# Expert biases loaded early, the last output tile in column halves, three low parts on VectorE, and a shorter way to the first expert

## The chip, the cores and the metric

The kernel runs on one core of a Trainium2 chip. The core has five engines with queues of their own: TensorE (PE), VectorE (DVE), ScalarE (ACT), GpSimd (POOL) and SyncE (SP, which here only issues transfers), and 16 DMA engines that serve all queues. The metric is the device time of one execution in microseconds (us). Of this kernel, runs agree within some 0.5%: three runs before the change took 1217.61, 1223.28 and 1223.31 us.

## The reference

One decoder layer on 256 tokens of width 1024, in float32:

```python
h = rms_norm(x, g_attn);  proj = h @ w_in
# proj -> native sparse attention (8 heads) and forgetting attention (8 heads)
y = merge[:, :, 0] * (o_nsa @ w_up_nsa) + merge[:, :, 1] * (o_fox @ w_up_fox)
x = x + y @ w_out
x = x + moe_ffn(rms_norm(x, g_mlp), ...)

def moe_ffn(...):                       # 32 experts, top 4 per token
    logits = xt @ w_router + b_router
    top_val, top_idx = top_k(logits, 4);  top_w = softmax(top_val)
    for each expert:                    # w_g, w_u, w_d are 1024 x 1024 each
        g = minimum(xt @ wg + bg, 7.0);  u = clip(xt @ wu + bu, -7.0, 7.0)
        y = ((u + 1.0) * g * sigmoid(1.702 * g)) @ wd + bd
        acc += combine[expert] * y
```

The expert weights are 32 x 3 matrices of 4 MB, 403 MB in all. Everything else that is read is some 35 MB.

## The kernel before, in words

The work is one long program for each engine, in an order written by hand; semaphores tie the engines together.

**Attention part (to about 250 us).** Every weight block is split into a high part (float32r, made by ACT, `keep_high`) and a low part (the rest, `keep_low`, line 357). A product is three TensorE passes: high by high, low by high, high by low. The low parts of the six projection blocks are made by POOL and DVE in turns. From the merge gates on, pieces are numbered (`MERGE`, `UP`, `OUT`), and their low parts are all made by POOL in the order of the numbers. `low_done(j)` is the semaphore value that says that the pieces below `j` have their low parts.

**Output product.** `y @ w_out` has eight pieces of the inner dimension (`OUT+0` to `OUT+7`), each for two tiles of 128 tokens (t = 0, 1) and two column halves (h = 0, 1); a piece of one tile is six matmuls with 512 columns (`out_piece`). Pieces 0 to 3 are done for both tiles; then pieces 4 to 7 for tile 0, then for tile 1. `w_hi` and `w_lo` hold four pieces, so ACT makes the high part of piece 4 only when TensorE has used piece 0 (`out_used`), and so on. Before `OUT+3` ACT issues eight transfers that bring the gate and up biases of the 32 experts (64 KB each) into `heads`, which is in use until then. After `OUT+7` ACT waits for them and makes `bias_hi`; DVE makes `bias_parts` from it and goes on to `x` only after that.

**From the output to the first expert.** DVE adds the output to `x` (line 1027), TensorE transposes the sums (`turn_rows`), DVE copies the transposes times a gain into `hT` (line 784), TensorE makes the router's logits (line 1457), ACT and POOL make the norm's factors and ACT scales `xn`. DVE then picks the top four (lines 1038 to 1062), TensorE counts with triangular matrices how many earlier tokens chose each expert (lines 1472 to 1476), DVE makes `route` and the one-hot matrices `hot`, and TensorE gathers the rows of the first two experts (`gather`, line 1486). Three calls of `keep_warm` put dummy matmuls (14, 10 and 4) ahead of steps that wait. Then DVE makes the number of rounds (`total_i`, `route_made`), reads it into a register (line 1179), and copies the gathered rows (`keep_x`, line 1159), on which the first expert's first product waits (`ex_made`).

**Experts.** For each expert TensorE does gate, up and down products, each in two halves of the inner dimension (`product`, line 1502), and scatters the rows back. Expert `it` begins with gate half 0; the down product of expert `it - 1` comes between the gate halves.

**Expert weights.** A half matrix is 2 MB. The 192 halves go through a ring of eight slots, issued by SP (line 408) in a fixed order. The first eight have no earlier expert to wait for, but the attention part uses the same slots, so `ex_freed` gives for each of these places what must be over: place 0 the turned outputs, place 1 `low_done(OUT)`, place 2 the merged `y`, place 3 `low_done(OUT + 4)`, place 4 `low_done(OUT + 8)`, places 5 to 7 the whole output product (`out_done` 2). Place 8 and all later ones wait until TensorE has used the slot: place 8 for half 0 of the first gate product.

Of the kernel before, what the change touches and what calls it, by code (L numbers as in the profile page):

```python
# [31 lines left out]
P = 128  # L32
# [11 lines left out]
E = 32  # L44
# [26 lines left out]
def build(nc, a, out):  # L71
    with ExitStack() as ctx:
# [3 lines left out]
        def sem(name):  # L76
            return ctx.enter_context(nc.semaphore(name))
# [50 lines left out]
        e_sel = sb("e_sel", [P, 2, 2 * C], F32R)  # L128
        sel_cols = sb("sel_cols", [P, 2, E])
# [40 lines left out]
        e_bias = heads[:, 1024:2048].rearrange("p (m n) -> p m n", m=2)  # L170
        bias_hi = oT_hi[:, 0:2].rearrange("p a b t -> p (a b t)").rearrange("p (m n) -> p m n", m=2)
        bias_parts = oT_lo[:, 0:2].rearrange("p a b t -> p (a b t)").rearrange("p (m n) -> p m n", m=2)
# [48 lines left out]
        rv0 = route[:, 0:8]  # L221
# [36 lines left out]
        bias_hi_made, bias_made, sel_ready, gain_in = map(sem, ("bias_hi_made", "bias_made", "sel_ready", "gain_in"))  # L258
        hotw_made, hotw_turned, hotT_made = sem("hotw_made"), sem("hotw_turned"), sem("hotT_made")
# [59 lines left out]

        def low_done(j):  # L320

            return (lo_made, j - N_SPLIT // 2)
# [6 lines left out]
        ex_freed = [(o_turned, 4), low_done(OUT), (y_made, KD), low_done(OUT + 4), low_done(OUT + KD)] + [(out_done, 2)] * 3  # L329
# [52 lines left out]
        def _(sp):  # L382
# [27 lines left out]
            def expert_head(first, end):  # L410

                for m, h in HEAD[first:end]:
                    sp.wait_ge(vrow_set, 1)
                    sp.wait_ge(*ex_freed[ex_place(m, h, 0, True)])
                    load_half(m, h, 0, ex_place(m, h, 0, True))

            def expert_body(base, u):

                it = base + u
                if isinstance(it, int):  # L420
                    e, e_before, now, prev = it, it - 1, it, it - 1
                else:
                    e = sp.snap(sp.to_reg(it & (E - 1)), min_val=0, max_val=E - 1)
                    e_before = sp.snap(sp.to_reg((it - 1) & (E - 1)), min_val=0, max_val=E - 1)
                    now, prev = sp.to_reg(it), sp.to_reg(it - 1)
                freed_by = [(half_done["up"], prev), (mat_done["up"], prev), (half_done["gate"], now),
                            (half_done["down"], prev), (mat_done["down"], prev), (mat_done["gate"], now)]
                for i, (m, h, back) in enumerate(BODY):
                    place = ex_place(m, h, u - back)
                    first = isinstance(it, int) and it == 1  # L430
                    if first and place < EX_SLOTS:
                        sp.wait_ge(*ex_freed[place])
                    elif first and (m, h) == ("up", 0):
                        sp.wait_ge(half_done["gate"], 1)
                    else:
                        sp.wait_ge(*freed_by[i])
                    load_half(m, h, e_before if back else e, place)
            for i, (name, pieces, k, n) in enumerate(BLOCKS):
                if name == "out1":
                    expert_head(0, 1)  # L440
                if name == "cv1":
                    sp.wait_ge(squared, NT)
                elif in_ring.index(name) >= len(RING):
                    for user in freed[in_ring[in_ring.index(name) - len(RING)]]:
                        sp.wait_ge(*user)
                if i:
                    load(name, pieces)

# [28 lines left out]
        def _(pool):  # L477
# [84 lines left out]
            for j in range(N_SPLIT, N_PIECES):  # L562
                keep_low(pool, nc.gpsimd, j, lo_made)
# [5 lines left out]
        def _(act):  # L569
# [189 lines left out]
        def _(dve):  # L759
# [250 lines left out]
            keep_low_y(KD - 1)  # L1010

# [9 lines left out]
            nc.vector.scalar_tensor_tensor(out=bias_parts, in0=bias_hi, scalar=less_hi[:, 0:1], in1=e_bias,  # L1021
                                           op0=ALU.mult, op1=ALU.add).then_inc(bias_made, 1)

            for t in range(NT):
                dve.wait_ge(out_done, 1 + t)
                for h in range(2):
                    last = nc.vector.scalar_tensor_tensor(out=x[:, t, 512 * h:512 * h + 512], in0=(S, TB)[t][h][:, :], scalar=0.5,
                                                          in1=x[:, t, 512 * h:512 * h + 512], op0=ALU.mult, op1=ALU.add)
                last.then_inc(summed, 1)
                keep_hT_tile(R_GM, [PJ[0], PJ[1], OB[0], OB[1]], 4, t)  # L1030
            for t in range(NT):
                dve.wait_ge(squared, NT + t + 1)
                inv_rms(rr[:, t:t + 1], ss[:, t:t + 1], D)


# [29 lines left out]
            dve.wait_ge(pos_done, 1)  # L1065
            for t in range(NT):
                last = nc.vector.scalar_tensor_tensor(out=above[:, t, :], in0=TB[1][:, E * t:E * t + E], scalar=1.0,
                                                      in1=chosen[:, t, :], op0=ALU.add, op1=ALU.mult)
            step(last)
# [5 lines left out]
            step(last)  # L1075
            for t in range(NT):
                for i in range(2):
                    last = nc.vector.tensor_scalar(hot[:, t, i, :], slot_no[:, :], rv0[:, 4 * i + t:4 * i + t + 1], None, ALU.is_equal)
                last.then_inc(hot_made, 1)
# [4 lines left out]
            step(nc.vector.tensor_reduce(tot[:, 0:1], TB[1][:, 2 * E:3 * E], AX.X, ALU.max))  # L1084
# [93 lines left out]
            dve.wait_ge(route_made, 1)  # L1178
            total = dve.value_load(total_i[0:1, 0:1], min_val=E, max_val=ROUNDS * E)
# [4 lines left out]
            expert(0, 0, True)  # L1184
            for u in range(1, STEPS):
                expert(u, u, False)
# [8 lines left out]
        def _(pe):  # L1195
# [233 lines left out]
            def out_piece(kk, t):  # L1429
                q, w = slice(P * t, P * t + P), quarter(OUT + kk)  # L1430
                for h in range(2):
# [12 lines left out]
            for t in range(NT):  # L1444
                for kk in range(4, KD):
                    if t == 0:
                        pe.wait_ge(*low_done(OUT + kk + 1))
                    elif kk == KD - 1:
                        pe.wait_ge(summed, 1)
                        turn_rows(x, 0, turned_banks)  # L1450
                    last = out_piece(kk, t)
                last.then_inc(out_done, 1)

            def router(t):

                for k in range(KD):
                    last = mm(PJ[0][:, E * t:E * t + E], hT[:, k, P * t:P * t + P], w_r[:, k, :], start=(k == 0), stop=(k == KD - 1))
                last.then_inc(lg_done, 1)
            pe.wait_ge(hT_made, 6)
            router(0)  # L1460
# [8 lines left out]
            keep_warm(14)  # L1469
# [4 lines left out]
            mm(TB[1][:, E:2 * E], before[:, :], chosen[:, 1, :], start=False, stop=True)  # L1474
            mm(TB[1][:, 2 * E:3 * E], ones[:, :], chosen[:, 0, :], start=True, stop=False)
            mm(TB[1][:, 2 * E:3 * E], ones[:, :], chosen[:, 1, :], start=False, stop=True).then_inc(pos_done, 1)
# [155 lines left out]
```

## Time and profile before

| | |
|---|---|
| runs before | 1217.61, 1223.28, 1223.31 us; median 1223.28 |
| profiled execution | 1221.0 us, span 1219.3 us |
| TensorE | busy 1123.5 us (92%), granted clock 0.986 of full |
| DVE, ACT, POOL | busy 430.5 (35%), 175.6 (14%), 133.0 us (11%) |
| DMA, slices 10 to 39 of 40 (305 to 1189 us) | 407 to 430 GB/s |
| DMA, slices 3 to 8 (91 to 244 us) | 69 to 162 GB/s |
| DMA, slices 9 and 10 (244 to 305 us) | 355 and 285 GB/s |
| chain that ended last | PE 48%, DMA 42%, DVE 7% |

The page cuts the span into 40 slices of 30.5 us. "Busy" of TensorE is pipelined and says little of its limit; the DMA rate by slice and the chain of waits say more. The profiled execution took 1.7 us more than its span.

### The profile page before, as it was taken

What the parts mean: (1) busy time and instruction counts of PE and PEld (TensorE: products, weight loads), DVE (VectorE), ACT (ScalarE), POOL (GpSimd) and SP (SyncE); (2) the same over time, 40 slices, a digit from 0 to 9 for tenths busy, and PEclk for the clock granted to TensorE, in tenths of its full rate; (3) what the DMA queues carried; (4) which work ended last, traced back from release to release, by engine and by line L of the source; (5) the groups of instructions that cost most, each with busy time, mean ns of one, the idle gap of its engine ahead of it and who ended that gap; (6) DMA issues with size and microseconds to landing.
All of it is one profiled execution on the core that took longest, in us unless ns stands there. A gap on an engine that the chain in (4) does not pass through costs nothing.

```text
span 1219.3 us, 14702 instructions
## 1 busy us (share of the span) xinstructions
PE 1123.5 (92%) x5812; PEld 543.6 (45%) x5812; DVE 430.5 (35%) x891; ACT 175.6 (14%) x363; POOL 133.0 (11%) x123
## 2 busy tenths in 40 slices
PE   4998999989999999999999999999999999999997
PEld 3776899866333343333333333333333333333332
DVE  4674575634232323223222322222322222222222
ACT  3452444422000000000000000000000000000000
POOL 4562344650000000000000000000000000000000
PEclk9997999999999999999999999999999999999999
DMA  8842232297999999999999999999999999999995
GB/s 268 274 162 69 70 120 89 81 355 285 415 407 428 428 428 427 428 428 428 427 429 430 427 428 427 429 430 429 426 427 429 429 430 428 427 428 429 429 430 233
DMA packets 49423, 438.81 MB, mean 360 GB/s; under 512 B 6538, under 2 KB 13774, under 8 KB 24814
## 3 DMA queue, kind: packets, MB, share of 16 engines
q1 hardware_dynamic: 47364, 437.44, 86.3%
q10 hardware_dynamic: 2026, 0.92, 0.3%
q8 instruction: 22, 0.36, 0.1%
q14 instruction: 11, 0.09, 0.0%
HBM read 437.30 MB, written 1.05 MB: 360 GB/s over the span
## 4 chain that ended last, share of the span: by engine, by line
PE 48%; DMA 42%; DVE 7%; issue 1%; ACT 1%; POOL 1%; SPq 1%; ACTq 0%; DVEq 0%
PE bank L1502 28%; DMA ring<-in_w_e_up_dram 20%; DMA ring<-in_w_e_gate_dram 20%; PE bank L1486 3%; PE bank L1516 2%; DVE w_lo L357 2%; DMA heads<-in_b_e_up_dram 1%; PE bank L1498 1%; PE bank L1372 1%; PE bank L1373 1%; PE bank L1371 1%; PE bank L1536 1%; PE bank L1340 1%; POOL small L549 1%; PE bank L1226 1%
## 5 line engine op out<-in xcount | busy, mean ns | idle before, releaser
L1502 PE MATMUL bank<-ring,hT 128*64 128x512 f32 x2048 | 466.9, 598 | 20.3 <-DMA ring<-in_w_e_gate_dram 19.5
L1502 PEld LDWEIGHTS bank<-ring,hT 128*64 128x64 f32 x2048 | 137.6, 136 | 302.2 <-issue 256.9
L1502 PE MATMUL bank<-ring,heads 128*64 128x512 f32 x1024 | 229.6, 601 | 0.6 <-DVE heads L1142 0.6
L1175 DVE TENSOR_TENSOR x<-x,bank 128x512 f32<-128x512 f32 x128 | 82.3, 684 | 143.9 <-PE bank L1516 143.9
L1502 PEld LDWEIGHTS bank<-ring,heads 128*64 128x64 f32 x1024 | 71.3, 138 | 136.9 <-issue 129.3
L1124 DVE TENSOR_SCALAR heads<-bank 128x512 f32<-128x512 f32 x32 | 22.1, 692 | 308.3 <-PE bank L1502 308.3
L357 POOL TENSOR_TENSOR w_lo<-ring,w_hi 128x512 fp32r<-128x512 f32 (+2 forms) x64 | 111.4, 1763 | 99.0 <-ACT w_hi L600 98.9
L733 ACT ACTIVATE work<-bank 128x256 f32<-128x256 f32 x32 | 12.3, 385 | 501.0 <-PE bank L1529 501.0
L1516 PE MATMUL bank<-heads,work 64*128 64x512 f32 x256 | 72.8, 641 | 1.5 <-ACT heads L738 0.8
L600 ACT ACTIVATE w_hi<-ring 128x512 fp32r<-128x512 f32 (+2 forms) x88 | 61.3, 723 | 29.6 <-PE bank L1235 16.1
L1486 PE MATMUL bank<-work,xn 128*128 128x128 f32 x528 | 64.5, 275 | 0.0
L1486 PEld LDWEIGHTS bank<-work,xn 128*128 128x128 f32 x528 | 61.6, 192 | 0.8 <-issue 0.8
L1498 PE MATMUL bank<-oT_lo,e_sel 128*128 128x512 f32 x64 | 31.6, 494 | 25.4 <-DMA ring<-in_w_e_gate_dram 22.1
L1142 DVE COPY heads<-bank 128x512 f32<-128x512 f32 x32 | 22.1, 692 | 90.1 <-PE bank L1536 90.1
L738 ACT ACTIVATE heads<-bank 128x512 f32<-128x512 f32 x32 | 19.1, 597 | 221.4 <-PE bank L1502 221.4
L1130 DVE TENSOR_SCALAR heads<-bank 128x512 f32<-128x512 f32 x32 | 22.1, 692 | 78.5 <-PE bank L1502 78.5
L1498 PEld LDWEIGHTS bank<-oT_lo,e_sel 128*128 128x128 f32 x64 | 11.9, 186 | 77.7 <-DMA ring<-in_w_e_gate_dram 29.0
L1516 PEld LDWEIGHTS bank<-heads,work 64*128 64x128 f32 x256 | 19.6, 184 | 53.9 <-issue 52.0
L745 ACT ACTIVATE heads<-heads 128x512 f32<-128x512 f32 x32 | 20.2, 630 | 152.8 <-DVE heads L1124 152.8
L1371 PE MATMUL bank<-hT_hi,w_hi 128*128 128x256 f32 x128 | 39.9, 311 | 0.0
L1372 PE MATMUL bank<-hT_lo,w_hi 128*128 128x256 f32 x128 | 36.9, 289 | 0.0
L1373 PE MATMUL bank<-hT_hi,w_lo 128*128 128x256 f32 x128 | 36.9, 288 | 0.0
(275 smaller groups left out, 1063.5 us busy)
## 6 DMA issues: line engine op xcount, KB each, us to landing
ring<-in_w_e_gate_dram SPq DMA_DIRECT2D x64, 2048.0 KB, 33.6
ring<-in_w_e_up_dram SPq DMA_DIRECT2D x64, 2048.0 KB, 35.2
ring<-in_w_e_down_dram SPq DMA_DIRECT2D x64, 2048.0 KB, 34.8
ring<-in_w_in_dram SPq DMA_DIRECT2D x8, 2048.0 KB, 7.9
ring<-in_w_out_dram SPq DMA_DIRECT2D x2, 2048.0 KB, 8.3
ring<-in_w_in_dram SPq DMA_DIRECT2D x2, 1024.0 KB, 9.0
ring<-in_w_ck_dram SPq DMA_DIRECT2D x1, 2048.0 KB, 8.5
heads<-in_w_cv_dram SPq DMA_DIRECT2D x1, 2048.0 KB, 14.1
```

The costliest lines, as they stand in the source:

```text
L357: last = vec.tensor_tensor(w_lo[:, k, n], w, w_hi[:, k, n], ALU.subtract)
L600: last = nc.scalar.activation(w_hi[:, k, n], w, ACT.Copy)
L1124: nc.vector.tensor_scalar(e_g, banks[1][:, :], LIMIT, None, ALU.min).then_inc(g_made, 1)
L1130: nc.vector.tensor_scalar(e_u, banks[2][:, :], LIMIT, -LIMIT, ALU.min, ALU.max).then_inc(up_read, 1)
L1175: ins = nc.vector.tensor_tensor(x[:, t, 512 * h:512 * h + 512], x[:, t, 512 * h:512 * h + 512], bank67[:, j % 2, :], ALU.add)
L1371: mm(PJ[c % 2][:, 0:T], w_hi[:, k, w], hT_hi[:, k, :], start=(k == 0), stop=False)
L1372: mm(PJ[c % 2][:, 0:T], w_hi[:, k, w], hT_lo[:, k, :], start=False, stop=False)
L1373: last = mm(PJ[c % 2][:, 0:T], w_lo[:, k, w], hT_hi[:, k, :], start=False, stop=(k == KD - 1))
L1486: last = mm(banks[0][:, P * k:P * k + P], xn[:, t, c:c + P], hot[:, t, :, :].rearrange("p u s -> p (u s)"), start=(t == 0), stop=(t == NT ...
L1498: mm(bank[:, :], e_sel[:, u % 2, :], bias_parts[:, (m == "up") * 1, :], start=True, stop=False)
L1502: last = mm(bank[C * half:C * half + C, :], lhs(kk), w[:, k, 512 * half:512 * half + 512], start=(kk == 0 and m == "down"), stop=(kk == KD ...
L1516: mm(bank67[:, h, :], hotT[C * h:C * h + C, t, :], e_y[C * h:C * h + C, :], start=True, stop=True).then_inc(spread_done, 1)
```

## The change

- The expert biases get a place of their own, `e_bias`, which shares its memory with `bias_parts`. SP issues their eight transfers behind the block `fk`, at some 35 us. ACT makes `bias_hi` after the high part of `OUT+5`, not after `OUT+7`.
- The low parts of `OUT+3`, `OUT+5` and `OUT+7` are made by DVE (between its other steps there), the rest by POOL. `low_done` and `ex_freed` name the right semaphores: place 3 now waits for POOL's and DVE's parts, and so does place 4.
- Tile 1 of the output is done in column halves: pieces 4 to 7 of half 0 (`last_half`), then the transposes of tile 0, then pieces 4 to 7 of half 1. DVE adds half 0 while TensorE works on half 1. The transposes and router products of tile 1 go by halves as well.
- `keep_warm` is called with 8, 3 and 2 dummy matmuls in place of 14, 10 and 4.
- `above` is made in one instruction, and `hot` from it in two, ahead of `route`. The count that only the number of rounds needs goes to another bank with a semaphore of its own (`load_counted`).
- TensorE no longer waits for `route_made` before the transposes of `comb`, and TensorE and DVE read the number of rounds after the first expert.

```diff
+        with ExitStack() as parts:
+            bias_parts = parts.enter_context(nc.sbuf_tensor("bias_parts", [P, 2, 512], F32R))
+        e_bias = sb("e_bias", [P, 2, 512])
...
+        LOW_BY_VECTOR = [OUT + 3, OUT + 5, OUT + 7]
+
         def low_done(j):
 
-            return (lo_made, j - N_SPLIT // 2)
+            piece, by_vector = j - 1, sum(v < j for v in LOW_BY_VECTOR)
+            if piece in LOW_BY_VECTOR:
+                return (lo_made_v, N_SPLIT // 2 + by_vector)
+            return (lo_made, j - N_SPLIT // 2 - by_vector)
...
-        ex_freed = [(o_turned, 4), low_done(OUT), (y_made, KD), low_done(OUT + 4), low_done(OUT + KD)] + [(out_done, 2)] * 3
+        ex_freed = [[(o_turned, 4)], [low_done(OUT)], [(y_made, KD)], [low_done(OUT + 3), low_done(OUT + 4)],
+                    [low_done(OUT + 7), low_done(OUT + 8)]] + [[(out_done, 2)]] * 3
...
+                if name == "fk":
+                    for q in range(4):
+                        for m, bias in enumerate(("b_e_gate", "b_e_up")):
+                            sp.dma_start(e_bias[E * q:E * q + E, m, :],
+                                         a[bias][0][:, 512 * (q // 2):512 * (q // 2) + 512]).then_inc(ebias_in, 16)
...
             for j in range(N_SPLIT, N_PIECES):
-                keep_low(pool, nc.gpsimd, j, lo_made)
+                if j not in LOW_BY_VECTOR:
+                    keep_low(pool, nc.gpsimd, j, lo_made)
...
             for kk in range(3, KD):
                 if kk == 3:
                     act.wait_ge(up_done, KD)
-
-                    for q in range(4):
-                        for m, name in enumerate(("b_e_gate", "b_e_up")):
-                            act.dma_start(e_bias[E * q:E * q + E, m, :],
-                                          a[name][0][:, 512 * (q // 2):512 * (q // 2) + 512]).then_inc(ebias_in, 16)
                 else:
                     act.wait_ge(out_used, kk - 3)
                 keep_high(OUT + kk)
-
-            act.wait_ge(ebias_in, 16 * 8)
-            nc.scalar.activation(bias_hi, e_bias, ACT.Copy).then_inc(bias_hi_made, 1)
-
-            for t in range(NT):
-                act.wait_ge(summed, t + 1)
+                if kk == 5:
+                    act.wait_ge(ebias_in, 16 * 8)
+                    nc.scalar.activation(bias_hi, e_bias[:, :, :], ACT.Copy).then_inc(bias_hi_made, 1)
+
+            for t in range(NT):
+                act.wait_ge(summed, (1, 3)[t])
                 square_rows(t)
...
+            keep_low(dve, nc.vector, OUT + 5, lo_made_v)
             dve.wait_ge(bias_hi_made, 1)
...
+            keep_low(dve, nc.vector, OUT + 7, lo_made_v)
...
+            dve.wait_ge(out_done, 1)
+            add_out(0, 0)
+            add_out(0, 1).then_inc(summed, 1)
+            dve.wait_ge(last_half, 1)
+            add_out(1, 0).then_inc(summed, 1)
+            out_banks = [PJ[0], PJ[1], OB[0], OB[1]]
+            keep_hT_tile(R_GM, out_banks, 4, 0)
+            dve.wait_ge(squared, NT + 1)
+            mean_of(0)
+            dve.wait_ge(out_done, 2)
+            add_out(1, 1).then_inc(summed, 1)
+            keep_hT_tile(R_GM, out_banks, 4, 1)
+            dve.wait_ge(squared, NT + 2)
+            mean_of(1)
+            dve.wait_ge(inv_made, n_inv[0])
...
+            for t in range(NT):
+                nc.vector.scalar_tensor_tensor(out=hot[:, t, :, :], in0=slot_no[:, :].unsqueeze(1).to_broadcast([P, 2, C]), scalar=1.0,
+                                               in1=above[:, t, 0:2].unsqueeze(2).to_broadcast([P, 2, C]),
+                                               op0=ALU.add, op1=ALU.is_equal).then_inc(hot_made, 1)
...
-            dve.wait_ge(route_made, 1)
-            total = dve.value_load(total_i[0:1, 0:1], min_val=E, max_val=ROUNDS * E)
             dve.wait_ge(gain_in, 16)
             keep_x(-1, -1)
             dve.wait_ge(comb_turned, 1)
             nc.vector.tensor_copy(combT, bank45[0:E, 1, T:2 * T].rearrange("p (t q) -> p t q", t=NT)).then_inc(combT_made, 1)
             expert(0, 0, True)
+            dve.wait_ge(route_made, 1)
+            total = dve.value_load(total_i[0:1, 0:1], min_val=E, max_val=ROUNDS * E)
...
+            for kk in range(4, KD):
+                pe.wait_ge(*low_done(OUT + kk + 1))
+                last = out_piece(kk, 0)
+            last.then_inc(out_done, 1)
+            for kk in range(4, KD):
+                last = out_piece(kk, 1, (0,))
+            last.then_inc(last_half, 1)
...
+            pe.wait_ge(summed, 1)
+            turn_sums(0, 0)
+            turn_sums(0, 1)
+            for kk in range(4, KD):
+                last = out_piece(kk, 1, (1,))
+            last.then_inc(out_done, 1)
...
             pe.wait_ge(summed, 2)
-            turn_rows(x, 1, turned_banks)
-            pe.wait_ge(hT_made, 8)
-            router(1)
+            turn_sums(1, 0)
+            router(0, 0)
+            pe.wait_ge(summed, 3)
+            turn_sums(1, 1)
+            router(0, 1).then_inc(lg_done, 1)
+            router(1, 0)
+            router(1, 1).then_inc(lg_done, 1)
...
-            keep_warm(14)
+            keep_warm(8)
...
-            keep_warm(10)
+            keep_warm(3)
             gather(2, 0, True)
             pe.wait_ge(comb_made, 1)
-            pe.wait_ge(route_made, 1)
...
-            keep_warm(4)
+            keep_warm(2)
             expert(0, 0, True)
+            pe.wait_ge(route_made, 1)
```

## Rows read from the trace of the kernel before

**Rows 1.** Windows: us, busy by engine, TensorE clock, DMA share, GB/s; steady stage.

```profile
356.00:576.00 220.00, 220.00 (x1053) 81.22 (x1049) 65.28 (x129) 13.75 (x26) 0.00 (x0) 1.00 1.00 427
```

**Rows 2.** The same view around the output product and the first expert.

```profile
252.00:268.00 16.00, 12.73 (x53) 9.26 (x52) 0.60 (x4) 4.96 (x5) 11.76 (x5) 1.00 1.01 356
...
294.00:296.00 2.00, 2.00 (x12) 0.43 (x7) 0.00 (x0) 0.00 (x0) 0.00 (x0) 1.00 0.00 0
```

**Rows 3.** Timeline of SP's queue: start us, us, line, transfer, count.

```profile
265.44 0.33 SPq L408 DMA_DIRECT2D ring<-in_w_e_gate_dram  x1
275.40 0.80 SPq L408 DMA_DIRECT2D ring<-in_w_e_down_dram  x2
...
296.21 6.82 SPq L408 DMA_DIRECT2D ring<-in_w_e_up_dram  x2
```

**Rows 4.** Timeline of ACT, output stage.

```profile
252.52 3.90 ACT L600 ACTIVATE w_hi<-ring 128x1024 fp32r<-128x1024 f32 x4 [3.30 <-issue]
...
269.25 1.06 ACT L714 ACTIVATE oT_hi<-heads 128x1024 fp32r<-128x1024 f32 x1 [8.97 <-DMA heads<-in_b_e_up_dram]
```

**Rows 5.** Timeline of POOL, output stage.

```profile
253.66 11.76 POOL L357 TENSOR_TENSOR w_lo<-ring,w_hi 128x1024 fp32r<-128x1024 f32 x5 [2.64 <-ACT w_hi L600]
```

**Rows 6.** Timeline of DVE, output stage.

```profile
242.00 2.52 DVE L996 TENSOR_TENSOR hT_lo<-heads,hT_hi 128x256 fp32r<-128x256 f32 x1
...
270.35 1.28 DVE L1021 SCALAR_TENSOR_TENSOR oT_lo<-oT_hi,less_hi,heads 128x1024 fp32r<-128x1024 f32 x1 [17.68 <-ACT oT_hi L714]
```

**Rows 7.** Timeline of TensorE, output stage.

```profile
246.17 0.40 PE L1434 MATMUL bank<-w_hi,hT_hi 128*128 128x512 f32 x1
...
254.13 0.39 PE L1436 MATMUL bank<-w_lo,hT_hi 128*128 128x512 f32 x1
256.18 0.47 PE L1434 MATMUL bank<-w_hi,hT_hi 128*128 128x512 f32 x1 [1.66 <-POOL w_lo L357]
...
272.89 1.09 PE L1203 MATMUL bank<-ident,x 128*128 128x128 f32 x8 [1.68 <-DVE x L1027]
```

**Rows 8.** Chain that ended last, router and dummy matmuls: start us, us, what.

```profile
275.37 1.71 PE bank L1457 x16
...
278.93 2.40 PE bank L1457 x16
281.33 4.40 PE bank L1468 x28
```

**Rows 9.** Timeline of DVE, expert choice.

```profile
281.45 0.41 DVE L1038 SCALAR_TENSOR_TENSOR work<-bank,small 128x32 f32<-128x32 f32 x2 [1.69 <-PE bank L1457]
...
283.92 0.23 DVE L1055 TENSOR_TENSOR work<-small,work 128x64 f32<-128x64 f32 x1
...
286.89 0.29 DVE L1067 SCALAR_TENSOR_TENSOR small<-bank,work 128x32 f32<-128x32 f32 x2 [1.77 <-PE bank L1476]
...
288.98 0.19 DVE L1084 TENSOR_REDUCE small<-bank 128x1 f32<-128x32 f32 x1
```

**Rows 10.** Timeline of TensorE, gather of the first two experts.

```profile
288.92 1.95 PE L1486 MATMUL bank<-work,xn 128*128 128x128 f32 x16
```

**Rows 11.** Chain that ended last, DVE ahead of the first expert, and the first products.

```profile
290.35 0.55 DVEq L1179
...
291.34 0.70 DVE hT L1159
...
292.08 0.50 PE bank L1498
```

**Rows 12.** Windows (columns of Rows 1) in which TensorE's clock was low.

```profile
110.00:112.00 2.00, 2.00 (x11) 2.00 (x11) 0.39 (x2) 0.00 (x0) 0.00 (x0) 0.50 0.00 0
...
280.00:282.00 2.00, 2.00 (x13) 2.00 (x13) 0.51 (x3) 2.00 (x2) 0.40 (x1) 0.57 1.00 426
```

**Rows 13.** Timelines of SP and ACT, projection stage.

```profile
35.00 11.98 SPq L388 DMA_DIRECT2D ring<-in_w_in_dram  x2
...
56.79 5.42 ACT L600 ACTIVATE w_hi<-ring 128x512 fp32r<-128x512 f32 x8 [8.53 <-PE bank L1235]
```

More of the change, by code:

```diff
@@ L431, in expert_body @@
                     if first and place < EX_SLOTS:
-                        sp.wait_ge(*ex_freed[place])
+                        for user in ex_freed[place]:
+                            sp.wait_ge(*user)
                     elif first and (m, h) == ("up", 0):
@@ L1010, in _ @@
             keep_low_y(KD - 1)
+            keep_low(dve, nc.vector, OUT + 3, lo_made_v)
             step(nc.vector.tensor_reduce(sel_cols[:, :, :], ident[:, :].rearrange("p (h q e) -> p h e q", h=2, q=2), AX.X, ALU.add))
@@ L1065, in _ @@
             dve.wait_ge(pos_done, 1)
+            step(nc.vector.scalar_tensor_tensor(out=above[:, :, :], in0=TB[1][:, 0:NT * E].rearrange("p (t e) -> p t e", t=NT),
+                                                scalar=1.0, in1=chosen, op0=ALU.add, op1=ALU.mult))
             for t in range(NT):
-                last = nc.vector.scalar_tensor_tensor(out=above[:, t, :], in0=TB[1][:, E * t:E * t + E], scalar=1.0,
-                                                      in1=chosen[:, t, :], op0=ALU.add, op1=ALU.mult)
-            step(last)
+                nc.vector.scalar_tensor_tensor(out=hot[:, t, :, :], in0=slot_no[:, :].unsqueeze(1).to_broadcast([P, 2, C]), scalar=1.0,
+                                               in1=above[:, t, 0:2].unsqueeze(2).to_broadcast([P, 2, C]),
+                                               op0=ALU.add, op1=ALU.is_equal).then_inc(hot_made, 1)
             steps = ROUNDS * E
@@ L1074, in _ @@
                                                col(round_off[:, :], E), ALU.add)
[L1075 to L1079, printed above, removed]
             for t in range(NT):
@@ L1427, in _, with out_piece @@
             turned_banks = [PJ[0], PJ[1], OB[0], OB[1]]
-            def out_piece(kk, t):
+            def out_piece(kk, t, halves=(0, 1)):
                 q, w = slice(P * t, P * t + P), quarter(OUT + kk)
-                for h in range(2):
+                for h in halves:
                     ps = (S, TB)[t][h][:, :].rearrange("p (a b) -> p a b", b=P)
@@ L1443, in _, with turn_sums, router @@
             pe.wait_ge(yT_lo_made, KD)
[L1444 to L1456, printed above, removed]
+            for kk in range(4, KD):
[5 more added lines that the diff above has]
+            last.then_inc(last_half, 1)
+            def turn_sums(t, j):
+                for k in range(4):
+                    c = P * (4 * j + k)
+                    last = nc.tensor.transpose(turned_banks[2 * t + j][:, P * k:P * k + P], x[:, t, c:c + P], ident[:, :])
+                last.then_inc(xn_turned, 1)
+            pe.wait_ge(summed, 1)
[4 more added lines that the diff above has]
+            last.then_inc(out_done, 1)
+            def router(t, j):
+                pe.wait_ge(hT_made, 4 + 2 * t + j + 1 if t else 6)
+                for k in range(4 * j, 4 * j + 4):
                     last = mm(PJ[0][:, E * t:E * t + E], hT[:, k, P * t:P * t + P], w_r[:, k, :], start=(k == 0), stop=(k == KD - 1))
-                last.then_inc(lg_done, 1)
-            pe.wait_ge(hT_made, 6)
-            router(0)
+                return last
             pe.wait_ge(summed, 2)
-            turn_rows(x, 1, turned_banks)
-            pe.wait_ge(hT_made, 8)
-            router(1)
+            turn_sums(1, 0)
[5 more added lines that the diff above has]
+            router(1, 1).then_inc(lg_done, 1)
             def keep_warm(n):
@@ L1473, in _ @@
             mm(TB[1][:, E:2 * E], ones[:, :], chosen[:, 0, :], start=True, stop=False)
-            mm(TB[1][:, E:2 * E], before[:, :], chosen[:, 1, :], start=False, stop=True)
-            mm(TB[1][:, 2 * E:3 * E], ones[:, :], chosen[:, 0, :], start=True, stop=False)
-            mm(TB[1][:, 2 * E:3 * E], ones[:, :], chosen[:, 1, :], start=False, stop=True).then_inc(pos_done, 1)
+            mm(TB[1][:, E:2 * E], before[:, :], chosen[:, 1, :], start=False, stop=True).then_inc(pos_done, 1)
+            mm(S[1][:, 0:E], ones[:, :], chosen[:, 0, :], start=True, stop=False)
+            mm(S[1][:, 0:E], ones[:, :], chosen[:, 1, :], start=False, stop=True).then_inc(load_counted, 1)
             def gather(n, half, newest):
```

27 lines of the change are left out of this document (12 added, 15 removed).

## The prediction, made before the change was run

> **What bounds the kernel now.** I read the DMA rates by slice first. From 305 us to the end the rate stands at 407 to 430 GB/s, while TensorE, at 92% busy, says little. The stage view of 356 to 576 us has both: TensorE without a gap and the DMA engines at a share of 1.00 and 427 GB/s [rows 1]. So a 2 MB half matrix takes 2.097 MB / 427 GB/s = 4.9 us, an expert of six halves 29.5 us, and 184 halves from place 8 on take some 904 us. The end hangs on when that stream starts and how long it then stands still; TensorE only follows it. This makes every microsecond by which the stream restarts earlier a microsecond of the result, and no work after the restart changes.
>
> Next, the view of SP's queue shows where the stream stands still. SP issues place 4 at 265.44, places 5 to 7 at 275.40 and the two behind, and place 8 at 296.21 [rows 3]. Three halves need 3 x 4.9 = 14.7 us, so the queue is empty again at some 292; in 294 to 296 us the share is 0.00 [rows 2]. What SP waits for at place 8 is the first half of expert 0's gate product. Thus the path that sets the end runs, before 296, over the engines: from the output product to that gate half.
>
> The chain of waits and the engines' timelines give that path. ACT begins the high part of `OUT+3` at 252.52, after 3.30 us of issuing [rows 4]; POOL makes the five last low parts in 11.76 us, 2.35 each [rows 5]; TensorE waits for them at 256.18 for 1.66 us and less later [rows 7]. ACT waits 8.97 us for the bias transfers, until 269.25, and DVE, behind it, 17.68 us until 270.35 [rows 4, 6]. TensorE waits for DVE's sum 1.68 us until 272.89 [rows 7]. Then follow router, choice, counts, gather, and DVE's copy at 291.34, on which the first product at 292.08 waits [rows 8 to 11].
>
> **The change, part by part.** I follow one path, output product to gate half 0, and give each step's new time. TensorE's start at 246.17 rests on steps that stay.
>
> *High parts.* ACT's transfers, 3.30 us of issuing, go; the high part of `OUT+3` starts at about 249.2 in place of 252.52. Each takes 3.90 / 4 = 1.0 us. The others wait for `out_used`: TensorE's 36 matmuls from 246.17 to 254.4 are 0.228 us each, so a piece of both tiles (12 matmuls) is 2.73 us, and pieces 0 to 3 end at 248.9, 251.6, 254.4 and 257.1 when nothing waits [rows 7]. The high parts of `OUT+4` to `OUT+7` are there at some 251.5, 252.8, 255.5 and 258.2, the bias's high part at 253.9.
>
> *Low parts.* DVE's price for one is not in this trace. The nearest row is its 1024-column instruction with two inputs in SBUF, 1.28 us [rows 6]; POOL's 2.35 is the other end. But DVE also stands: at 242.00 an instruction of 256 columns took 2.52 us while POOL worked on a low part of 1024 columns [rows 6]. I take 1.28 and let each wait for the other's whole instruction. DVE does `OUT+3` at 251.6 to 252.8 (behind its last `yT` low part); POOL `OUT+4` to 255.3; DVE `OUT+5` to 256.5; POOL `OUT+6` to 258.9; DVE the bias parts to 260.1 and `OUT+7` to 261.3. The page "SBUF — State Buffer" of the Trainium skill, section "Who interferes with whom", says that a VectorE instruction with two SBUF inputs and a GpSimd one that reads SBUF shut each other out for whole instructions. Row and rule agree on DVE's side; the rule speaks against this part of the change: without it `OUT+7` would be there at 259.5, with it at 261.3.
>
> *Output product.* TensorE needs `OUT+4` at 257.1, `OUT+5` at 258.5, `OUT+6` at 259.8 and `OUT+7` at 261.2. Only the last is late, by 0.2. Tile 0 ends at 262.8. Half 0 of tile 1 (12 matmuls, 2.73), eight transposes (1.09) and half 1 (2.73) follow without a wait, since DVE's two additions are over at 264.2: the whole product ends at 269.35. Before, it ended with SP's issue at 275.40 [rows 3]. This is 6.0 earlier. Of DVE's price the bounds are: 0.7 less cost gives 0.2, 2.35 with the lock 1 to 3 us later.
>
> *Router.* Eight transposes 1.09 and 32 passes at 1.71 for 16 make 4.5, so the logits can be read at 273.95. DVE's additions and copies of tile 1 end at 272.2 and hide behind the router; the factor of tile 1 is there at 272.9. Before, the second router block took 2.40 rather than 1.71, and it waited for `hT` [rows 8]; DVE read at 281.45 [rows 9]. 7.5 earlier.
>
> *Choice and counts.* From 281.45 to the end of line 1055 are 2.7 us, so `chosen` is there at 276.7. The 28 passes of dummies, 4.40 us from 281.33, kept TensorE until 285.7, 1.5 beyond that point [rows 8, 9]. Eight calls are 16 passes of 0.11 to 0.16, over at 275.7 to 276.4: the wait for them goes. Six passes of counts take 0.75, and DVE begins `above` at 277.65, behind `comb`; before 286.89. 9.2 earlier. `hot` now stands ahead of `route` (0.6 us saved) and takes two instructions for four: done at 278.7. `xn` is done at 275.4 and hides. TensorE's three dummies end at 278.7 as well. The gather of 1.95 runs 278.7 to 280.7; before it began at 288.92 [rows 10]. 10.2 earlier.
>
> *To the first product.* DVE still has `route` and the chain of small instructions to do, 1.05 and the 1.37 between 288.98 and 290.35, which ends at 281.1; the register read of 0.9 us between 290.35 and 291.34 goes from here [rows 9, 11] and lies in DVE's free time behind expert 0. The copy takes 0.70, so the first product starts at 281.9 in place of 292.08: 10.2 earlier. What is late next is DVE's chain, by 0.3 over the gather.
>
> *The transfers.* Gate half 0 ends at 286.0, and place 8 is issued there and not at 296.21. Places 5 to 7, issued at 269.4, are served until 286.0, by the 16.6 us from issue to the empty queue of before. So the stream has caught up just when place 8 comes: the DMA engines bound the gain at about 11. The early issue of biases costs SP the 3.3 us of issuing that ACT spent [rows 4], behind `fk`, at 35.0, and SP has nothing to issue until 46.6; the high part of `fk` starts at 56.79 [rows 13]. Even 4 us later `fk` would be there. Cost nothing; without that cover, up to 4. Their leaving the output stage gives more: 252 to 268 us ran at 356 and not 427 GB/s [rows 2], (1 - 356/427) x 16 = 2.7 us of transfer time, which is what lets places 5 to 7 find a free queue.
>
> *Sum.* 1221.0 us of the profiled execution (span 1219.3 and 1.7 around it) less 10.2 is 1210.8; I say 1211. The median of the runs is 2.3 above that execution and the fastest 3.4 below, and I keep this spread in the range.
>
> **The rivals.**
>
> *The clock falls in the first expert.* At 280 to 282 us the granted clock was 0.57 [rows 12], after gaps of TensorE at 272 and 278 (the router waits in rows 7 and 8): 1.2 GHz for part of the time and 2.4 for the rest. Fewer dummies leave gaps at 276 and 281. Such a low stretch of some 3 us on counts, gather and gate half would add 1 to 3 us: 1212 to 1214. For it: the dummies fall from 28 to 13 calls. Against: TensorE has no gap from 246 to 276 now. The Trainium skill's "TensorE: Matmul & The Clock Gate", in "Part 1: The HAM clock gate", adds that the point at which the clock changes varies from run to run; that would put this between runs of one kernel.
>
> *The output product gains less.* If DVE and POOL hold each other up by more than I let them, TensorE waits for `OUT+5` and `OUT+7`, 3 to 4 us in all; the gain is 6 to 7: 1214 to 1215. For it: the 2.52 us row.
>
> *The stream has its start from something else.* If the still times at 274 and 294 us were filled later by slack, TensorE and not DMA would bound and the time stay near 1220. Against: a share of 1.00 from 356 on.
>
> *Slower.* With fewer dummies the clock might stay at half, as it did around 110 us with TensorE three quarters busy (clock 0.50) [rows 12]. At half clock a stretch of length L loses L/2. The gain of 10.2 is gone at L = 20 us, and from 33 us on the kernel is slower by 6: 1227. This decides in the first two experts. Against: there the clock was 1.00 in 294 to 296 us [rows 2] on the same products.
>
> *Better than forecast.* The low stretch of 280 to 284 us goes and nothing takes its place, and DVE's low parts cost below 1.28: 1207 to 1209.
>
> **How the numbers follow.** A difference under 0.5% (6 us) is what a measurement of this kernel can't tell from none. Forecast 1208 to 1214: 0.55. Clock in the first expert: 0.18. Less from the output: 0.09. Start from something else: 0.07. Slower: 0.05. Better: 0.06. Of these, faster by over 0.5% are the forecast, most of the clock case, the better one and a part of the lesser output: 0.81; the rest but 0.05 is within. The range is 1204 to 1218: the cases from 1207 to 1215 with the runs' spread of +2.3 and -3.4.
>
> **What would show it.** In the changed kernel's profile: no ACT wait on the biases; `out_done` at 269 to 270 by SP's issue of places 5 to 7; logits read near 274; gather near 279; first product near 282; place 8 issued near 286, with no or one short hole in the transfers ahead of it; clock 1.00 from 246 to 300. The forecast is wrong if the first product is early by 10 and the end isn't, or if `OUT+5` and `OUT+7` hold TensorE.

## The result, and the profile after

The changed kernel took 1212.48 us in the median of nine runs, against 1227.36 us for nine runs of the kernel before on the same chips; the ratio of their means is 0.989 with a 95% interval of 0.987 to 0.992, that is 13 us (10 to 17) less; the two medians are 14.9 us apart. The forecast was 1211 us, from a sum of 10.2 us less. Later runs of the kernel before had medians of 1224.6 to 1225.6 us.

The profiled execution took 1214.83 us, its span 1213.1. First the queue of SP, which answers to [rows 3]: start us, us, line, transfer.

```profile
264.23 0.33 SPq L415 DMA_DIRECT2D ring<-in_w_e_gate_dram  x1
272.34 0.81 SPq L415 DMA_DIRECT2D ring<-in_w_e_down_dram  x2
...
288.31 6.82 SPq L415 DMA_DIRECT2D ring<-in_w_e_up_dram  x2
...
347.61 0.33 SPq L415 DMA_DIRECT2D ring<-in_w_e_gate_dram  x1
```

Place 8 goes out at 288.31, 7.9 us earlier than in [rows 3], and the span is 6.2 shorter. But TensorE began the output product at 249.46 and not at 246.17, and not through the change, as far as the runs show: the two executions are 1.1 us apart at 14 us and 2.1 at 28, ahead of the moved transfers, and over all profiles the start is at 247.2 us in the mean of nine with early biases and at 247.1 in five without. What the change touches runs from there to place 8: 50.0 us before, 38.85 after, 11.2 less. From place 8 to the end it is 923.1 and 924.8 us. I measure each kernel in these three pieces.

Next the timelines of ACT, DVE, POOL and TensorE in the output stage (brackets: idle time before, and what ended it), against [rows 4 to 7].

```profile
254.17 2.03 ACT L615 ACTIVATE w_hi<-ring 128x1024 fp32r<-128x1024 f32 x2 [0.71 <-DMA ring<-in_w_out_dram]
256.10 1.04 ACT L724 ACTIVATE oT_hi<-e_bias 128x1024 fp32r<-128x1024 f32 x1
```

```profile
254.85 1.21 DVE L364 TENSOR_TENSOR w_lo<-ring,w_hi 128x1024 fp32r<-128x1024 f32 x1
...
256.74 1.81 DVE L1028 CAST e_sel<-sel_cols 128x128 fp32r<-128x128 f32 x2
258.46 1.21 DVE L364 TENSOR_TENSOR w_lo<-ring,w_hi 128x1024 fp32r<-128x1024 f32 x1
259.60 3.42 DVE L1033 SCALAR_TENSOR_TENSOR bias_parts<-oT_hi,less_hi,e_bias 128x1024 fp32r<-128x1024 f32 x1
262.94 1.21 DVE L364 TENSOR_TENSOR w_lo<-ring,w_hi 128x1024 fp32r<-128x1024 f32 x1
266.01 1.29 DVE L1038 SCALAR_TENSOR_TENSOR x<-bank,x 128x512 f32<-128x512 f32 x2 [1.86 <-PE bank L1459]
```

```profile
255.31 3.02 POOL L364 TENSOR_TENSOR w_lo<-ring,w_hi 128x1024 fp32r<-128x1024 f32 x1 [1.00 <-ACT w_hi L615]
258.99 2.94 POOL L364 TENSOR_TENSOR w_lo<-ring,w_hi 128x1024 fp32r<-128x1024 f32 x1 [0.67 <-ACT w_hi L615]
```

```profile
268.54 1.03 PE L1479 MATMUL bank<-ident,x 128*128 128x128 f32 x8
...
276.47 2.03 PE L1505 MATMUL bank<-ones,ident 128*128 128x128 f32 x16
279.50 0.41 PE L1509 MATMUL bank<-work,before 128*128 128x32 f32 x2 [1.00 <-DVE work L1080]
...
281.38 1.95 PE L1523 MATMUL bank<-work,xn 128*128 128x128 f32 x16
```

ACT has its biases without a wait, DVE makes a low part in 1.21 us, and the last is over at 264.15, just ahead of TensorE. DVE now waits for TensorE at 266.01; in [rows 4, 6] it was ACT and DVE that were late. TensorE stands nowhere from 249.46 to 278.5. It then waits 1.00 us for the choice, until 279.50, and no longer keeps the choice waiting.

The stage views (columns as in [rows 1]) show the transfers and the clock.

```profile
252.00:268.00 16.00, 16.00 (x72) 13.28 (x71) 13.30 (x14) 7.14 (x8) 8.26 (x3) 1.00 1.00 427
...
272.00:274.00 2.00, 2.00 (x20) 1.91 (x19) 1.29 (x2) 0.93 (x1) 0.00 (x0) 1.00 0.57 131
...
288.00:290.00 2.00, 2.00 (x18) 1.80 (x16) 0.00 (x0) 0.00 (x0) 0.00 (x0) 1.00 0.72 205
...
360.00:576.00 216.00, 216.00 (x1034) 79.98 (x1032) 65.78 (x130) 12.89 (x24) 0.00 (x0) 1.00 1.01 428
```

The 16 us that ran at 356 GB/s in [rows 2] run at 427; of the two holes ahead of the steady stream, short ones are left. The clock stays at full from the output product to the first expert, where [rows 12] had 0.57. (In the profiles of two kernels of the next section that follow the same path, the one with work in the loop and the one for expert 2, it was 0.76 and 0.77 in 270 to 275 us, and their path is 0.4 us longer.)

### The profile page after: what moved, and what is told of

It reads as the page before. It is cut to its first block, busy times and chain, and to the rows that moved or that the text cites. A ratio compares the mean times of both kernels' runs of the same rounds, so it can differ in the third digit from the quotient of the medians.

```text
span 1213.1 us, 14640 instructions
## 1 busy us (share of the span) xinstructions
PE 1120.7 (92%) x5782; PEld 540.8 (45%) x5782; DVE 437.1 (36%) x891; ACT 175.6 (14%) x363; POOL 127.1 (10%) x120
## 4 chain that ended last, share of the span: by engine, by line
PE 50%; DMA 41%; DVE 6%; issue 1%; POOL 1%; ACT 1%; SPq 1%; DVEq 0%; ACTq 0%
PE bank L1539 28%; DMA ring<-in_w_e_up_dram 20%; DMA ring<-in_w_e_gate_dram 20%; PE bank L1523 3%; PE bank L1553 2%; DVE w_lo L364 2%; PE bank L1535 1%; PE bank L1394 1%; PE bank L1396 1%; PE bank L1395 1%; PE bank L1573 1%; PE bank L1363 1%; POOL small L563 1%; PE bank L1249 1%; PE bank L1424 1%
## 5 line engine op out<-in xcount | busy, mean ns | idle before, releaser
L364 POOL TENSOR_TENSOR w_lo<-ring,w_hi 128x512 fp32r<-128x512 f32 (+2 forms) x61 | 105.6, 1749 | 100.1 <-ACT w_hi L615 100.1
L1535 PE MATMUL bank<-bias_parts,e_sel 128*128 128x512 f32 x64 | 31.9, 499 | 25.6 <-DMA ring<-in_w_e_gate_dram 22.2
L1535 PEld LDWEIGHTS bank<-bias_parts,e_sel 128*128 128x128 f32 x64 | 11.9, 186 | 78.0 <-DMA ring<-in_w_e_gate_dram 29.1
## 6 DMA issues: line engine op xcount, KB each, us to landing
ring<-in_w_in_dram SPq DMA_DIRECT2D x2, 1024.0 KB, 10.2
```

Source lines behind the costliest of these rows:

```text
L364: last = vec.tensor_tensor(w_lo[:, k, n], w, w_hi[:, k, n], ALU.subtract)
L1535: mm(bank[:, :], e_sel[:, u % 2, :], bias_parts[:, (m == "up") * 1, :], start=True, stop=False)
```

## The experiments

All ratios are to the kernel before on the same chip, with 95% intervals. The ratio of the changed kernel is the 0.989 (0.987 to 0.992) above. "Path" is from TensorE's first matmul of the output product to SP's issue of place 8, in the profiled execution: 38.85 us in the changed kernel, 39.25 in both of the others that don't differ from it there. Each kernel but the one before (three) has one profile, so a path is one execution's, and what the ratios can't tell apart rests on the rows of that execution. From place 8 to the end the profiles take 924.5 to 925.7 us, with four exceptions: 923.1 (the kernel before, first profile, and the one with 28 dummy calls), 922.6 (expert 2) and 927.7 (the delay).

**Biases late again.**

```diff
-                if name == "fk":
-                            sp.dma_start(e_bias[E * q:E * q + E, m, :],
...
                 if kk == 3:
                     act.wait_ge(up_done, KD)
+                            act.dma_start(e_bias[E * q:E * q + E, m, :],
...
-                if kk == 5:
-                    act.wait_ge(ebias_in, 16 * 8)
+            act.wait_ge(ebias_in, 16 * 8)
```

> The changed kernel, with one part undone: ACT again issues the eight bias transfers ahead of the high part of OUT+3 and makes their high part after OUT+7; DVE makes bias_parts after the low part of OUT+7. My theory: ACT's 3.3 us of issuing and the wait for the transfers (DVE at x only near 20 us after the issue) make the output product end 5 to 7 us later, and the slower transfers cost the stream up to 2.7: 5 to 8 us slower than the changed kernel, so still 5 to 8 faster than before. Rival: the early biases were hidden anyway and the gain comes from the other parts: less than 2 us slower than the changed kernel.

Measured: ratio 0.999 (0.997 to 1.001), path 49.1. With every other part in place, nothing that is clear of noise is left of the gain. ACT, TensorE and two stages of this kernel:

```profile
271.60 1.06 ACT L723 ACTIVATE oT_hi<-e_bias 128x1024 fp32r<-128x1024 f32 x1 [11.31 <-DMA e_bias<-in_b_e_up_dram]
```

```profile
275.22 1.97 PE L1478 MATMUL bank<-ident,x 128*128 128x128 f32 x8 [6.16 <-DVE x L1037]
```

```profile
254.00:270.00 16.00, 13.19 (x56) 9.98 (x54) 8.10 (x8) 4.73 (x5) 4.85 (x2) 1.00 1.01 358
274.00:276.00 2.00, 0.78 (x4) 0.78 (x5) 1.76 (x3) 0.80 (x1) 0.00 (x0) 0.50 0.04 16
```

The last of the eight transfers of 64 KB lands 18 us after its issue (the median one after 12 to 13) and holds ACT and, behind it, DVE; TensorE stands 6.16 us, until 275.22, and from 272 to 278 its clock is at half, which doubles the eight transposes (1.97 against 1.03 us). My theory had the wait but not the clock: 10.3 us on the path, not 5 to 8, and all of it ahead of SP's issue of places 5 to 7.

**Low parts on POOL again.** `LOW_BY_VECTOR = []`, and DVE's three calls left out.

> The changed kernel with all eight low parts of the output product on POOL again. My theory: five low parts in a row at 2.5 us each from the high part of OUT+3 put OUT+7 some 2 us behind TensorE's need: 1.5 to 3 us slower than the changed kernel. Rival: DVE and POOL shut each other out (DVE's low part waits for POOL's whole instruction), and the split gives nothing: within 0.5 us of the changed kernel, or faster.

Measured: ratio 0.993 (0.990 to 0.995), path 42.0: 3.1 us longer, just over what I expected, and all of it inside the output product. The ratio's interval overlaps that of the changed kernel, so the loss is shown by the trace and not by the times. POOL makes six in a row, 2.60 each, and TensorE waits for them (0.68 us at 259.00, 1.64 at 262.30):

```profile
246.68 15.57 POOL L364 TENSOR_TENSOR w_lo<-ring,w_hi 128x1024 fp32r<-128x1024 f32 x6 [1.76 <-ACT w_hi L615]
```

**Tile 1 in whole pieces again.**

> The changed kernel with tile 1 of the output product in whole pieces again, the transposes of tile 0 ahead of its last piece, and the sums, transposes and router blocks in the order of before. My theory: from the end of the output product to the logits 5.9 us and not 4.3: 1.5 to 2.5 us slower than the changed kernel. Rival: DVE's and ACT's work behind the last sum hides behind something else: no difference.

The edit: pieces 4 to 7 of tile 1 with both halves, the transposes of tile 0 ahead of piece 7, and DVE and ACT in the old order. Measured: ratio 0.994 (0.992 to 0.997), path 43.7: 4.8 longer; the intervals of the ratios just touch. The logits come 6.6 us after SP's issue of places 5 to 7, and not 4.4: 2.2 us, within the 1.5 to 2.5 that I expected. The rest, 2.6 us between logits and first product, is again the clock, low behind a wait of 0.94 us for `hT`:

```profile
275.00:280.00 5.00, 5.00 (x26) 5.00 (x25) 3.27 (x17) 3.54 (x4) 0.00 (x0) 0.50 1.03 442
```

**Dummy calls.** 14, 10 and 4 again; and, in another kernel, none.

> The changed kernel with 14, 10 and 4 dummy calls again in place of 8, 3 and 2. My theory: at the full clock a call takes 0.24 us; the 14 end 0.5 us behind the choice, the 10 hold the gather back by 1.9, the 4 the first product by up to 0.5: 2 to 3 us slower. Rival: they keep the clock up in the first experts (0.50 to 0.73 at 338 to 346 us in the changed kernel) and so pay for themselves: no difference, or 1 to 2 us faster.

> The changed kernel without any dummy call between router and first expert. My theory: TensorE then stands some 2 us ahead of the counts, 0.5 ahead of the gather and 0.8 ahead of the first product; the clock may fall in the first expert, as it does in other places behind such gaps: 1 to 3 us slower than the changed kernel. Rival: the gaps are too short to matter and the calls cost more than they keep: 0 to 1 us faster.

Measured: 28 calls, ratio 0.992 (0.989 to 0.995), path 40.5, 1.6 longer; no call, ratio 0.993 (0.991 to 0.995), path 41.4, 2.6 longer. By their paths both lose; the two intervals overlap that of the changed kernel. The 28 calls hold the gather back by 1.6 us, less than the 2 to 3 of my theory, and in this execution the part behind place 8 was 1.7 us shorter than in the changed kernel, so that its span was no longer. That is what my rival said, but the kernel before has the same 28 calls and took 923.1, 924.7 and 924.5 us there in three executions: whether the calls give anything back stays open. Without calls, TensorE and the stage behind it:

```profile
279.31 0.64 PE L1508 MATMUL bank<-work,before 128*128 128x32 f32 x2 [2.86 <-DVE work L1080]
```

```profile
280.00:285.00 5.00, 4.84 (x23) 4.73 (x24) 2.83 (x15) 0.00 (x0) 0.00 (x0) 0.50 1.00 429
```

A gap of 2.86 us, half clock on the counts, and the gather takes 3.75 us and not 1.95: here the path bears out the theory of 1 to 3 us. By these single executions the 13 calls of the change stand between a cost that they take and one that they avoid.

**The two parts alone, on the kernel before.** Early biases, with the kernel's old order otherwise; and the three low parts on DVE.

> The kernel before with the early biases alone (own place, issued by SP behind fk, high part after OUT+5, bias_parts in DVE's order of before). My theory: the parts aren't additive; here POOL's five last low parts in a row (11.8 us) take over from the bias wait, so the output product gets 3 to 4 us shorter, and the low clock at 280 to 284 us may go (1 to 2): 3 to 6 us faster than before. Rival: the biases cost what their undoing cost the changed kernel (10.3 us on the path from the output product to place 8): 9 to 11 us faster than before.

> The kernel before with DVE making the low parts of OUT+3, OUT+5 and OUT+7, and nothing else of the change. My theory: TensorE gets through tile 0 up to 4 us earlier and then stands at the sums all the longer, for DVE is still held by the bias transfers: path from the output product's start to place 8 as before, within 1 us; the time within 1.5 us of before. Rival: the parts are additive, and this gives the 3.2 us that its undoing cost the changed kernel.

Measured: early biases alone, ratio 0.996 (0.994 to 0.997), path 48.4; low parts alone, ratio 1.004 (1.001 to 1.006), path 58.1, which is slower than before. So the early biases alone give 5 us of time, within the 3 to 6 that I expected, where their undoing costs 10 us of path; POOL's low parts in a row take over, and TensorE waits 0.69 and 1.65 us for them. The low parts alone are a loss of 4 us (2 to 7), where their undoing costs 3. They bring TensorE to the sums 2 us earlier, and there it stands 4.70 us instead of 1.68 [rows 7], with this stage behind it:

```profile
278.81 1.97 PE L1215 MATMUL bank<-ident,x 128*128 128x128 f32 x8 [4.70 <-DVE x L1039]
```

```profile
290.00:295.00 5.00, 5.00 (x24) 5.00 (x25) 1.96 (x11) 4.39 (x4) 0.55 (x1) 0.50 0.99 426
```

In this execution the clock stayed at half from 278 to some 298 us: router, choice and counts all took longer. It was the slowest of this kernel's twelve (1235.74 us, median 1228.99), so its path shows more than the kernel usually loses. That TensorE was faster ahead of a fixed wait made the wait longer; that the longer wait made the slow stretch longer fits, but one profile doesn't show it. My theory of no change fell; so did additivity.

**Does the restart of the stream set the end?** 36 more dummy calls ahead of the first product; and 16 calls in every fourth expert from expert 4 on.

> The changed kernel with 36 more dummy calls (0.24 us each, 8.6 us) on TensorE right ahead of the first expert's first product. My theory: the restart of the weight stream sets the end, so the whole 8 to 9 us come back in the time. Rival: TensorE is ahead of the transfers and has slack, or the end hangs on something else: less than 4 us.

> The changed kernel with 16 dummy calls (3.8 us) on TensorE in every fourth expert from expert 4 on, seven times, 27 us of TensorE work in all. My theory: from 356 us on the transfers bound and TensorE has 2.7 us of slack in each expert, so nothing of it is seen, or up to 2 us where the first of them holds a slot back: 0 to 2 us slower than the changed kernel. Rival: TensorE bounds the experts: over 10 us, up to 27.

Measured: the delay, ratio 0.996 (0.994 to 0.997), path 46.8, 8.0 longer, and 8 us (4 to 12) slower than the changed kernel by the ratios. The profiled execution, at 1223.95 us, is 4.3 above the median of its kernel, and 2.9 of that lies behind place 8 (927.7 against 924.8). While TensorE works on the dummies no transfer runs (stage below), and that is never given back. The 27 us in the loop: ratio 0.987 (0.986 to 0.989), no slower than the changed kernel, TensorE busier by 20 us from 576 us on (589.04 against 569.24) and the rate the same.

```profile
290.00:295.00 5.00, 5.00 (x29) 2.24 (x28) 0.00 (x0) 0.00 (x0) 0.00 (x0) 1.00 0.00 0
```

```profile
576.00:1190.00 614.00, 589.04 (x2870) 227.65 (x2868) 171.72 (x338) 33.81 (x63) 0.00 (x0) 1.00 1.01 428
```

Work of TensorE counts one for one ahead of the restart and, at 3.8 us in every fourth expert from expert 4 on, nothing behind it.

**The hole at expert 2.** In the changed kernel TensorE waits 1.38 us in `bias_rows`, the clock is at half from 339 to 345, and the queue runs empty before the issue at 347.61:

```profile
340.00:345.00 5.00, 5.00 (x10) 1.33 (x10) 1.28 (x2) 0.00 (x0) 0.00 (x0) 0.50 1.01 429
345.00:350.00 5.00, 5.00 (x26) 1.61 (x24) 0.00 (x0) 0.00 (x0) 0.00 (x0) 0.97 0.57 187
```

```diff
-                    if t:
-                        pe.wait_ge(bd_added, t)
                     for h in range(2):
-                        last = mm(bank67[:, h, :], combT[:, t, :], ...)
+                        last = mm(banks[2 + h][:, :] if t == 0 else bank67[:, h, :], combT[:, t, :], ...)
```

> The changed kernel with the down biases' rows of tile 0 (expert 2) made in two banks of their own, so that TensorE does tile 1 without waiting for DVE's additions. My theory: in the changed kernel the 1.38 us wait at 337 us is followed by half clock from 339 to 345, and SP then issues the next half only at 347.6, behind an empty queue (90 GB/s in 346 to 348 us); without the wait the hole shrinks by 2 to 4 us and the kernel is that much faster than the changed one. Rival: the hole is filled later by TensorE's slack or has another cause: no difference.

The same stage without the wait:

```profile
340.00:345.00 5.00, 5.00 (x26) 1.68 (x24) 0.00 (x0) 0.60 (x1) 0.00 (x0) 1.00 1.00 423
345.00:350.00 5.00, 5.00 (x25) 1.48 (x23) 1.98 (x3) 0.63 (x1) 0.00 (x0) 1.00 1.03 439
```

The hole and the low clock are gone, and from place 8 to the end it takes 922.6 us, the shortest of all profiles (the changed kernel 924.8, the one with work in the loop 925.7). But it is only 0.5 us below the first profile of the kernel before, which has the same wait of 1.38 us in front of the same four matmuls and ran them at nearly full clock. The kernel before, then the changed one:

```profile
346.77 2.04 PE L1581 MATMUL bank<-heads,work 32*128 32x512 f32 x4 [1.38 <-DVE x L1167]
338.89 3.77 PE L1618 MATMUL bank<-heads,work 32*128 32x512 f32 x4 [1.38 <-DVE x L1190]
```

The ratio is 0.988 (0.986 to 0.989) and the median 1209.69 us; the kernel with work in the loop, which keeps the wait, had 1209.92 beside it on the same chip. So the trace shows 0.5 to 3 us, by the execution that it is held against, and the times show none: whether this version beats the changed kernel stays open.

**The kernel before, twice more.**

> The kernel before, once more, for the profile: its profiled execution took 1221.0 us and the median of its runs near 1225. My theory: an execution differs from another in when the output product starts (244.3 to 249.5 us in ten profiles) and in the low-clock stretches of the first three experts (place 8 to end 923 to 928 us), and the path between, 50.0 us, stays within 2. Rival: the path between is itself as variable, and the 11.2 us gained on it are partly chance.

> The kernel before, a second time, with the same theories as for the first: start of the output product at 244 to 250 us, 50 us (within 2) to place 8, 923 to 928 us from there to the end.

Measured: 1226.81 and 1220.84 us. The output product began at 248.3 and 242.5 us, the path was 52.0 and 52.1, and 924.7 and 924.5 us were left. In both the clock is low behind the wait for the sums, in the stage that was at full clock in the first profile; of the first:

```profile
275.00:280.00 5.00, 4.56 (x22) 4.14 (x22) 2.27 (x4) 1.15 (x2) 0.00 (x0) 0.66 0.03 10
```

So the path of the kernel before varies by 2 us, as much as my theory allowed, and the profile of [rows 7, 8] was of its shorter kind; that it varies as much as the start of the output product (6 us), the rival, did not come. From the 52.0 us of these two profiles to the 38.85 to 39.25 of the changed path it is 13 us. That the ratio says 13.1 as well is closer than its interval (10 to 17) can vouch for.

## Why the prediction was right, and where its sizes were off

*What bounds.* Right, and shown by the delay and the work in the loop.

*The path's steps.* From the start of the output product, forecast and measured: to its end 23.2 and 22.7; on to the logits 4.6 and 4.6; to the gather 4.8 and 4.6; to the first product 3.2 and 2.8; to place 8 4.1 and 4.1. Sum 39.8 and 38.85. No step fails; TensorE met no late low part, though I had given the last 0.2. What each part is worth is shown by undoing for the biases, the low parts, the halves of tile 1 and the dummies. The shorter way from choice to first product (`above` in one instruction, `hot` ahead of `route`, the later register read) was not undone by itself: with 28 calls in both kernels, logits to gather took 6.3 us in the changed one and 7.5 to 7.9 before, so these parts are worth some 1.2 to 1.6 us there, and 0.3 from gather to first product.

*High and low parts.* The high part of `OUT+4` waited 0.71 us for its weights, which I hadn't priced; nobody waited for it. DVE's low part took 1.21 us (forecast 1.28). That DVE and POOL shut each other out is there in both directions: POOL's instruction takes 3.02 and 2.94 us against 2.48 for the same form while DVE doesn't hold it up, and `bias_parts` takes 3.42 against 1.28 in [rows 6]. I let the two small casts of `e_sel` go free; they took 1.81 us against 0.36 before, and 4.0 where POOL worked without a break (low parts on POOL again). The section of "SBUF — State Buffer" in the Trainium skill that the prediction draws on counts `cast` among the instructions that can contend; the runs agree, and my step had missed it. It cost nothing, as TensorE needed that low part later.

*The early biases.* Cost nothing, as forecast: SP issued them from 37.5 to 42 us and its next load at 48.71. What they are worth I had not priced as a part of its own. It is the largest: 10.3 us of path when it alone is undone, 5 us of time when it alone is made.

*The transfers.* Places 5 to 7 and place 8 meet as forecast, with short holes at 272 and 288 us.

*The size.* The term that was mis-sized is the start of the sum. I took 50.0 us of path from one execution, where the two others took 52.0 and 52.1. Of the 2 us, 0.4 are the biases, which landed later (the transposes began 27.1 us after the start of the output product, against 26.7), and 1.5 are TensorE at half clock behind the wait for them; the execution that I had read escaped this stretch, while all three had another one between 280 and 290 us. So 10.2 became 13. That 1211 came out so near 1212.48 is in part luck: the profiled 1221.0 that I started from lay 4 us below the usual median (1225), the gain that I took off was 3 us too small, and the two cancel. For the profiled executions, 1210.8 + 3.3 (later start) + 1.7 (after place 8) - 1.0 (path) is the 1214.8 that was measured.

*The rivals.* The clock in the first expert stayed at full: the rival of 0.18 did not come. Without any dummies a low stretch comes just ahead of it (2.6 us of path). The output product gained as forecast. The slower rival, a long stretch at half clock, came in a kernel with one part of the change alone, at 278 to 298 us, and there behind a wait for the biases and not behind fewer dummies.

## What to carry to other kernels

Where a stream of transfers bounds the rest, price a change by the moment at which the stream restarts, and add up only the chain to that moment; work behind it is free while it stays within the slack (here 27 us of it in seven experts cost nothing). Look for small transfers that an engine waits for in the middle of such a chain: eight of 64 KB, asked for where they were needed, cost more (10.3 us of path) than three matrix splits on the wrong engine (3.1). A part of a change that shortens what leads up to a wait can be worth nothing until the wait is gone, and here it was worth less: judge them together, and undo each from the whole as well as adding it alone.

## What the runs showed of the hardware

- In or behind a wait of TensorE the granted clock often fell to half, and what followed took up to twice as long: with 6.16 us of wait, 0.50 in 274 to 276; with 4.70, 0.50 from 278 to 297; with 2.86, 0.50 in 280 to 285; with 1.38 at expert 2, 0.50 in 340 to 345. No length of wait divides the cases: one of 0.94 us (whole pieces) had a low stretch behind it, one of 1.00 us (the changed kernel) none, and 270 to 275 us had 0.76 and 0.77 in two kernels that had no wait there. The same wait of 1.38 us stands ahead of the same four matmuls in 13 of 14 profiles, and they took from 1.98 to 3.78 us. The kernel before had a low stretch behind the wait for the sums in two of three executions, and one between 280 and 290 us in all three.
- Executions of the same program differ in when a stage far from the change begins: the output product of the kernel before at 242.5, 246.2 and 248.3 us. What sets it is open. Over all kernels the start lies between 242.5 and 251.1 us. One profile against another of the same kernel can be 6 us off by that alone.
- Eight transfers of 64 KB beside the 2 MB ones brought the rate to 356 to 358 GB/s for 16 us, against 427 without them; the last of them landed 17 to 18 us after its issue, the median one after 12 to 13. In the changed kernel, issued at 37 us, they took 8.
